# A hybrid recurrent, attention and Fourier stack on one core: scan normalisation by tokens, and dilated keys in sorted order

## The chip, the cores and the metric

The kernel runs on one core of a Trainium2 chip. The metric is the device time of the whole program in microseconds, from launch to the last store. TensorE multiplies matrices, VectorE, ScalarE and GpSimd do the rest, and SyncE queues transfers. The program is one long row of stages; each is a block of five instruction streams, one an engine, that wait for one another through semaphores. A stage starts on all engines when the one before has ended on all of them.

## The reference, cut to what matters

A first block on 2048 tokens of width 1024 (recurrent branch plus dilated attention), then a second block of two layers, on 2048 tokens and 256 context tokens. The change touches two computations.

The dilated attention has 8 heads of 64 channels and three patterns. Each works on every dilation-th token, in windows of 128 of those:

```python
DILATED_PATTERNS = ((128, 1), (512, 4), (2048, 16))
outs, lses = zip(*[dilated_attention(qh, kh, vh, w, d) for (w, d) in DILATED_PATTERNS])
wts = jax.nn.softmax(jnp.stack(lses, axis=0), axis=0)
att = jnp.einsum('pbhs,pbhsd->bhsd', wts, jnp.stack(outs, axis=0))
```

The scans of the second block (4 heads of 64 channels) end with a root-mean-square norm over each head's 64 channels, a gain, and a gate:

```python
def rms_norm_2(x, g):
    y = xf * lax.rsqrt(jnp.mean(xf * xf, axis=-1, keepdims=True) + EPS)
    return (y * g.astype(jnp.float32)).astype(x.dtype)
...
gain = hg_g.reshape(HG_HEADS, 1, HG_DV)
out_l = from_heads(rms_norm_2(o_lat, gain)).astype(q_l.dtype)
...
y = jnp.concatenate([y_conv, att_l * g_att, hg_l * g_hg, y_four], axis=-1) @ w_out
```

## The kernel before

Features lie on the 128 partitions, tokens along the free axis: `QT` and `KTt` (tiles `q_t` and `k_t` in the trace) are [128, 4, 2048], four pairs of heads, one head in each half of the partitions.

**stage_dilated** (lines 874 to 1127) works through `plan`, 96 units in a fixed order: 3 patterns x 16 query tiles of 128 x 2 groups of four heads. Units 0 to 31 are the pattern of dilation 1, 32 to 63 that of 4, 64 to 95 that of 16. A unit has `w` = 1 or 2 key blocks: two except for the first tile of each row of blocks, so 30, 24 and 0 units of the three patterns are 256 keys wide, the others 128. TensorE's order for unit u is written out: transpose the probabilities of u (`turn`, L1000), score matmuls of u + 2 (`scores`, L986), two matmuls of the second block's modulation (`modulate`, L1030), probabilities times values of u (`values`, L1017). In `scores` the queries are the stationary operand and the keys the moving one; both are read with the dilation as the step. VectorE masks and takes minima (L1058), copies transposed probabilities (L1068), adds modulation rows (L1078) and copies results out of PSUM (L1089) and, in every second unit, the statistics (L1088). ScalarE takes exponentials (L1111) and copies the other half of the transposes (L1121). GpSimd has no work. SyncE loads values (L935) and modulation weights (L942), stores result rows (L964) and modulation rows (L948), and brings back the recurrent branch's result into `yaT` (tile `ya_t`, L970), needed in the next stage only.

**stage_hgrn_norm** (lines 1930 to 1983) runs once in each layer, after the two scans. It cuts the output `oT` of [128, 2, tokens] into units of 512 tokens (`CH`): ten in layer 0, two of which have 256 tokens, and eight in layer 1. Per unit: ScalarE squares (L1949), TensorE multiplies by `headmean` (a 128x128 matrix of two 64x64 blocks of 1/64), which gives each channel its head's mean (L1964), ScalarE takes the root (L1956), VectorE the reciprocal (L1971) and the product with output and gain (L1973), GpSimd the product with the gate (L1981). Squares, roots and the PSUM tiles have two buffers each. The next stage begins with the projection of L2054.

## Time and profile before

| | us |
|---|---|
| three timed runs: median (lowest, highest) | 5314.19 (5302.58, 5317.26) |
| the profiled execution, and its span | 5306.81, 5304.8 |
| TensorE busy, share of the span | 4750.0, 90% |
| VectorE, ScalarE, GpSimd busy | 2483.5, 1688.8, 1208.3 |
| dilated attention, from and to | 808, 1223 |
| norm of the scans, layer 0, from and to | 2108, 2149 |
| norm of the scans, layer 1, from and to | 4031, 4068 |

The trace gives each instruction's start, duration and engine; an fp32 matmul shows as two weight loads (PEld) and two matmuls (PE). Ends of matmuls are modelled, so the pace of a row of them is read from one group's start to the next group's start, which is exact, and not from their durations, which overlap. A busy share says little by itself; what ends an engine's wait says more. The granted clock is TensorE's, as a share of 2.4 GHz: 1.00 is that level and 0.50 the lower one of 1.2 GHz.

### The profile page before, as it was taken

How to read it: one execution, taken by the hardware profiler on the slowest of the kernel's cores; microseconds unless marked ns; L12 is line 12 of the kernel's file. 1: busy time of each engine (PE TensorE's matmuls, PEld its weight loads, DVE VectorE, ACT ScalarE, POOL GpSimd, SP SyncE). 2: the span in 40 equal slices, each digit the busy share in tenths (PEclk: the TensorE clock that was granted, in tenths of full speed). 3: DMA queues.
4: the chain of work that ended last, by engine and by line, in shares of the span. 5: the costliest groups of instructions: out<-in, count | busy, mean ns of one | idle time of the engine just before them, and what ended most of it. 6: DMA issues, size and time to landing. Idle time of an engine off the chain costs nothing. (4 is left out here: it accounts for less than half of the span.)

```text
span 5304.8 us, 66741 instructions
## 1 busy us (share of the span) xinstructions
PE 4750.0 (90%) x26209; PEld 3269.9 (62%) x26209; DVE 2483.5 (47%) x4843; ACT 1688.8 (32%) x3122; POOL 1208.3 (23%) x1239
## 2 busy tenths in 40 slices
PE   6989998997969988899999898989896999988989
PEld 3447776775758655745554576876665644544767
DVE  3322345556643656635541264444566445501544
ACT  3332225553353111223441233242112234321431
POOL 1000020003410101418880001001122267830000
PEclk8989999998979999899999999999998999999999
DMA  5012104334420000100001202200000100002022
GB/s 190 8 56 72 40 1 158 133 104 162 149 99 17 1 9 1 57 17 11 11 9 38 72 16 92 88 28 17 9 1 31 36 9 13 7 25 86 16 72 95
DMA packets 149818, 272.41 MB, mean 51 GB/s; under 512 B 11645, under 2 KB 82693, under 8 KB 147845
## 3 DMA queue, kind: packets, MB, share of 16 engines
q1 hardware_dynamic: 145188, 257.67, 14.3%
q10 hardware_dynamic: 4320, 10.49, 0.5%
q8 instruction: 211, 3.46, 0.3%
q14 instruction: 99, 0.80, 0.1%
HBM read 198.92 MB, written 69.19 MB: 51 GB/s over the span
## 5 line engine op out<-in xcount | busy, mean ns | idle before, releaser
L1489 PE MATMUL ps_proj<-features_high,weights_high 128*128 128x512 f32 (+1 forms) x880 | 347.2, 394 | 60.6 <-DVE features_low L1552 31.2
L1489 PE MATMUL ps_proj<-features_high,weights_low 128*128 128x512 f32 (+1 forms) x880 | 341.1, 388 | 0.0
L1489 PE MATMUL ps_proj<-features_low,weights_high 128*128 128x512 f32 (+1 forms) x880 | 340.2, 387 | 0.0
L1703 PE MATMUL ps_s<-qf,kb 64*128 64x128 f32 x3264 | 235.7, 285 | 60.9 <-DVE scores_t L1873 55.5
L2436 ACT ACTIVATE weight_ring<-ps_st 128x1024 f32<-128x1024 f32 x193 | 197.9, 1025 | 249.1 <-PE ps_st L2323 243.2
L1703 PEld LDWEIGHTS ps_s<-qf,kb 64*128 64x128 f32 x3264 | 200.8, 188 | 112.6 <-issue 59.8
L1552 DVE TENSOR_TENSOR features_low<-h_t,features_high 128x1024 fp32r<-128x1024 f32 (+1 forms) x140 | 159.8, 1144 | 186.7 <-ACT features_high L1517 186.4
L2941 PE MATMUL ps_o<-w_out_high,y_high 128*128 128x512 f32 x544 | 217.4, 400 | 27.4 <-DVE y_low L2959 19.9
L1489 PEld LDWEIGHTS ps_proj<-features_high,weights_high 128*128 128x128 f32 x880 | 171.6, 195 | 110.0 <-DVE weights_low L1543 31.3
L2484 DVE TENSOR_REDUCE features_or_outputs<-ps_max 128x2 f32<-128x1024 f32 x128 | 156.7, 1224 | 166.0 <-PE ps_max L2293 166.0
L728 PE MATMUL ps_proj<-weights_high,features_high 128*128 128x512 f32 x512 | 207.0, 404 | 27.8 <-DVE features_low L823 27.8
L2466 POOL TENSOR_TENSOR features_or_outputs<-features_or_outputs,weight_ring 128x512 f32<-128x512 f32 x176 | 223.4, 1290 | 33.3 <-ACT weight_ring L2436 30.9
L2466 POOL TENSOR_TENSOR y_t<-y_t,weight_ring 128x512 f32<-128x512 f32 x176 | 223.3, 1290 | 33.3 <-ACT weight_ring L2436 30.9
L2484 DVE TENSOR_REDUCE y_t<-ps_max 128x2 f32<-128x1024 f32 x128 | 156.7, 1224 | 156.3 <-PE ps_max L2293 156.3
L1552 DVE TENSOR_TENSOR features_low<-features_or_outputs,features_high 128x1024 fp32r<-128x1024 f32 (+1 forms) x120 | 144.2, 1204 | 169.6 <-ACT features_high L1517 169.3
L1111 ACT ACTIVATE scores<-scores,row_stats 128x256 f32<-128x256 f32 (+1 forms) x384 | 172.4, 450 | 160.5 <-DVE row_stats L1058 160.5
L2941 PE MATMUL ps_o<-w_out_low,y_high 128*128 128x512 f32 x544 | 214.3, 394 | 0.0
L2941 PE MATMUL ps_o<-w_out_high,y_low 128*128 128x512 f32 x544 | 214.0, 393 | 0.0
L2318 PE MATMUL ps_st<-q_high,k_split 128*128 128x512 f32 x580 | 211.5, 446 | 0.0
L1873 DVE COPY_PREDICATED scores_t<-level_masks,ps_s 128x256 f32<-128x256 uint8 (+1 forms) x432 | 210.2, 560 | 0.0
L1517 ACT ACTIVATE features_high<-h_t 128x1024 fp32r<-128x1024 f32 (+1 forms) x140 | 136.1, 974 | 221.7 <-PE ps_proj L1489 190.7
L728 PE MATMUL ps_proj<-weights_high,features_low 128*128 128x512 f32 x512 | 204.8, 400 | 0.0
(428 smaller groups left out, 10542.7 us busy)
## 6 DMA issues: line engine op xcount, KB each, us to landing
weight_ring<-in_w_in_dram SPq DMA_DIRECT2D x40, 1024.0 KB, 5.6
weight_ring<-in_w_mod_dram SPq DMA_DIRECT2D x48, 512.0 KB, 4.1
t_rows<-t_rows SPq DMA_DIRECT2D x64, 256.0 KB, 2.3
x_res<-h_rows SPq DMA_DIRECT2D x32, 512.0 KB, 3.5
res<-result SPq DMA_DIRECT2D x48, 264.0 KB, 2.1
res_rows<-res SPq DMA_DIRECT2D x48, 264.0 KB, 3.8
h_t<-v_rows SPq DMA_DIRECT2D x3, 4096.0 KB, 13.9
q_rows<-q_rows SPq DMA_DIRECT2D x34, 256.0 KB, 2.6
```

Of the source, the lines that this page charges most:

```text
L728: mm = pe.matmul(out[:, :], f_[:, k, i * P:(i + 1) * P], w_[:, k0 + k, :], start=(k0 + k == 0 and n == 0), stop=(k0 + k == KT - 1 and n == 2))
L1111: act.activation(pr[:, u % 2, 2 * b + j, 0:w * P], sc[:, u % 2, 2 * b + j, 0:w * P], ACT.Exp, bias=stat[:, (u // 2) % 4, h:h + 1], scale=-1.0,
L1489: mm = pe.matmul(bank[:, 0:n], w_[:, k0 + k, i * P:(i + 1) * P], f_[:, k, 0:n], start=start, stop=stop)
L1517: act.activation(self.fh[:, s % NB, :, 0:n], self.hT[:, k0:k0 + KS, c0:c0 + n], ACT.Copy).then_inc(self.fhs.h, 1)
L1552: dve.tensor_tensor(self.fl[:, s % NB, :, 0:n], self.hT[:, k0:k0 + KS, c0:c0 + n], self.fh[:, s % NB, :, 0:n].bitcast(F32), ALU.subtract). ...
L1703: mm = pe.matmul(pS[pr][h][:, i * P:(i + 1) * P], kb[lo, s % 2, pr, i * P:(i + 1) * P], q, start=True, stop=True)
L1873: ins = dve.copy_predicated(dst, mask, src)
L2318: pe.matmul(sT[b][:, kv, :], KA[:, kv, ks], QA[g % 2][:, kv, :, :].rearrange("p i c -> p (i c)"), start=True, stop=False)
L2436: act.activation(pT[s % 3], sT[s % 2][:, :, :], ACT.Exp, scale=HD ** -0.5).then_inc(ex.h, 1)
L2466: pool.tensor_tensor(acc[g % 2][:, kv, :], before, pT[s % 3][:, kv, :], ALU.add).then_inc(pa.h, 1)
L2484: ins = dve.tensor_reduce(part[:, g % 2, t, c, :].rearrange("p (v i) -> p v i", v=2)[:, :, i], pM[:, :, 0:n], AXX, ALU.max)
L2941: mm = pe.matmul(ps[i % 2][half][:, :], y[:, i % 2, k, :], w[:, k, sl], start=(k == 0 and n == 0), stop=(k == KT - 1 and n == 2))
```

## The change

In **stage_dilated** GpSimd copies the keys into another order: for the pattern of dilation 4 from `KTt` into `yaT`, which is free at that time, with all tokens of one remainder next to one another; for dilation 16 from there back into `KTt`. `scores` reads a contiguous run of the sorted keys; the queries are read with a step, as before. TensorE waits for the first four copies ahead of unit 32 and for all eight ahead of unit 64. GpSimd waits with the second four for the last scores of dilation 1. The four loads into `yaT` move to units 69, 73, 77 and 81.

In **stage_hgrn_norm** the squares become the stationary operand and two columns of `headmean` the moving one, so that a matmul gives the means of 128 tokens, tokens on partitions, one column a head. All means of one channel pair (`pr`) go into one PSUM tile; one root and one reciprocal serve them all. ScalarE widens each value to 64 columns (`o_repeat`), and products with the identity put them back with channels on partitions. VectorE's multiply reads them from PSUM. The loops interleave the second pair's means with the first pair's spreading.

```diff
-                if u % 8 == 1 and 1 <= u // 8 <= CT:
-
-                    c = u // 8 - 1
+                c = u // 4 - NT - 1
+                if u % 4 == 1 and 0 <= c < CT:
+
+                    sp.wait_ge(kp.h, kp.at(8))
                     sp.dma_start(yaT[:, c, :], ya_d[:, c, :]).then_inc(yld.h, 16)
...
                 p, t, hh, (q0, dil), (k0, _), w, vt = plan[u]
+                if p >= 1 and u % (2 * NT) == 0:
+                    pe.wait_ge(kp.h, kp.at(4 * p))
+                k1 = (k0 % dil) * (S // dil) + k0 // dil
...
                                        QT[lo:lo + HD, pair, q0:q0 + dil * (P - 1) + 1:dil],
-                                       KTt[lo:lo + HD, pair, k0:k0 + dil * (w * P - 1) + 1:dil], start=True, stop=True)
+                                       KS[p][lo:lo + HD, pair, k1:k1 + w * P], start=True, stop=True)
...
+        @block.gpsimd
+        def _(pool):
+            for pr in range(4):
+                pool.tensor_copy(yaT[:, pr, :].rearrange("p (r i) -> p r i", r=4),
+                                 KTt[:, pr, :].rearrange("p (i r) -> p r i", r=4)).then_inc(kp.h, 1)
+
+            pool.wait_ge(smm.h, smm.at(2 * NT))
+            pool.wait_ge(kp.h, kp.at(4))
+            for pr in range(4):
+                pool.tensor_copy(KTt[:, pr, :].rearrange("p (a r i) -> p r a i", a=4, r=4),
+                                 yaT[:, pr, :].rearrange("p (r i a) -> p r a i", r=4, a=4)).then_inc(kp.h, 1)
...
 def stage_hgrn_norm(env, layer, oT, zT, chunks):
...
+        rr = env.sb(ctx, "o_rms", [P, 2, TN, 2])
+        re = env.sb(ctx, "o_repeat", [P, 2, CH // P, 2, HD])
+        pm = env.banks(ctx, "ps_mean", 2)
+        ps = env.banks(ctx, "ps_on", 4)
...
+        heads = env.headmean[:, 0:P:HD]
...
+            def root(pr):
+                act.wait_ge(mm_.h, mm_.at((pr + 1) * NC))
+                act.activation(rr[:, pr, :, :].rearrange("p t h -> p (t h)"), pm[pr][:, 0:2 * TN], ACT.Sqrt,
+                               bias=env.eps[:, :]).then_inc(rt.h, 1)
...
+            def repeat(u):
+                pr, (c0, n) = units[u]
+                m = n // P
+                act.wait_ge(rc.h, rc.at(pr + 1))
+                if u >= 2:
+                    act.wait_ge(bc.h, bc.at(u - 1))
+                act.activation(re[:, u % 2, 0:m, :, :].rearrange("p t h c -> p (t h) c"),
+                               rr[:, pr, c0 // P:c0 // P + m, :].rearrange("p t h -> p (t h)")[:, :, None].to_broadcast([P, 2 * m, HD]),
+                               ACT.Copy).then_inc(ex.h, 1)
+
+            for u in range(NC + 1):
+                square(u)
+            root(0)
+            for u in range(NC):
+                if NC + 1 + u < NU:
+                    square(NC + 1 + u)
+                repeat(u)
+            root(1)
+            for u in range(NC, NU):
+                repeat(u)
...
+            def means(u):
+                pr, (c0, n) = units[u]
                 pe.wait_ge(sq.h, sq.at(u + 1))
+                for j in range(n // P):
+                    t = c0 // P + j
+                    mm = pe.matmul(pm[pr][:, 2 * t:2 * t + 2], o2[:, u % 2, j * P:(j + 1) * P], heads, start=True, stop=True)
+                mm.then_inc(mm_.h, 1)
+
+            def spread(u):
+                pr, (c0, n) = units[u]
+                pe.wait_ge(ex.h, ex.at(u + 1))
+                if u >= 4:
+                    pe.wait_ge(sd.h, sd.at(u - 3))
+                for j in range(n // P):
+                    mm = pe.matmul(ps[u % 4][:, j * P:(j + 1) * P],
+                                   re[:, u % 2, j, :, :].rearrange("p h c -> p (h c)"), env.ident[:, :],
+                                   start=True, stop=True)
+                mm.then_inc(bc.h, 1)
...
             for u, (pr, (c0, n)) in enumerate(units):
+                if u % NC == 0:
+                    dve.wait_ge(rt.h, rt.at(pr + 1))
+                    dve.reciprocal(rr[:, pr, :, :], rr[:, pr, :, :]).then_inc(rc.h, 1)
                 o = oT[:, pr, c0:c0 + n]
-                dve.wait_ge(rt.h, rt.at(u + 1))
-                dve.reciprocal(rr[:, u % 2, 0:n], rr[:, u % 2, 0:n]).then_inc(rc.h, 1)
-                dve.wait_ge(rc.h, rc.at(u + 1))
+                dve.wait_ge(bc.h, bc.at(u + 1))
                 dve.scalar_tensor_tensor(out=o, in0=o, scalar=gains[:, 2 * layer + pr:2 * layer + pr + 1],
-                                         in1=rr[:, u % 2, 0:n], op0=ALU.mult, op1=ALU.mult).then_inc(sd.h, 1)
+                                         in1=ps[u % 4][:, 0:n], op0=ALU.mult, op1=ALU.mult).then_inc(sd.h, 1)
```

TensorE in the norm stage of layer 0, before (`ps_on` is the PSUM tile of the means, `o_sq` the squares):

```order
4050 L1958 UNCONDITIONAL_BRANCH
4051 L1964 MATMUL ps_on_146<-o_sq,head_mean 128x512 x4
4052 L1964 MATMUL ps_on_146<-o_sq,head_mean 128x256
4053 L1964 MATMUL ps_on_146<-o_sq,head_mean 128x512 x4
4054 L1964 MATMUL ps_on_146<-o_sq,head_mean 128x256
```

TensorE at the same place, after:

```order
4051 L2008 MATMUL ps_mean_147<-head_mean,o_sq 128x2 x30
4052 L2017 MATMUL ps_on_148<-ident,o_repeat 128x128 x4
4053 L2008 MATMUL ps_mean_147<-head_mean,o_sq 128x2 x4
4054 L2017 MATMUL ps_on_148<-ident,o_repeat 128x128 x4
4055 L2008 MATMUL ps_mean_147<-head_mean,o_sq 128x2 x2
4056 L2017 MATMUL ps_on_148<-ident,o_repeat 128x128 x28
```

Ten matmuls become 36 two columns wide and 36 of 128 columns; 30 of the former stand ahead of the first spreading product.

VectorE in the same stage, before (the first of ten such pairs):

```order
2076 L1971 RECIPROCAL o_rms<-o_rms 128x512
2077 L1973 SCALAR_TENSOR_TENSOR features_or_outputs<-features_or_outputs,vcols,o_rms 128x512
2078 L1971 RECIPROCAL o_rms<-o_rms 128x512
2079 L1973 SCALAR_TENSOR_TENSOR features_or_outputs<-features_or_outputs,vcols,o_rms 128x512
2080 L1971 RECIPROCAL o_rms<-o_rms 128x512
```

VectorE there, after:

```order
2076 L2036 RECIPROCAL o_rms<-o_rms 128x36
2077 L2039 SCALAR_TENSOR_TENSOR features_or_outputs<-features_or_outputs,vcols,ps_on_148 128x512 x4
2078 L2039 SCALAR_TENSOR_TENSOR features_or_outputs<-features_or_outputs,vcols,ps_on_148 128x256
2079 L2036 RECIPROCAL o_rms<-o_rms 128x36
2080 L2039 SCALAR_TENSOR_TENSOR features_or_outputs<-features_or_outputs,vcols,ps_on_148 128x512 x4
2081 L2039 SCALAR_TENSOR_TENSOR features_or_outputs<-features_or_outputs,vcols,ps_on_148 128x256
```

Ten wide reciprocals become two of 36 columns; the multiplies stay, with another second operand.

SyncE's queue in the dilated attention, before, around the first load into `ya_t` (units 7 to 11):

```order
60 L942 DMA weight_ring<-in_w_mod_dram 128x4x256
61 L964 DMA res<-result 128x528
62 L970 DMA ya_t<-ya_rows 128x2048
63 L942 DMA weight_ring<-in_w_mod_dram 128x4x256
64 L948 DMA mod_rows<-mod_rows 1x256 x4
```

SyncE's queue after, around the same load, now among the units of dilation 16:

```order
136 L944 DMA weight_ring<-in_w_mod_dram 128x4x256
137 L966 DMA res<-result 128x528
138 L973 DMA ya_t<-ya_rows 128x2048
139 L944 DMA weight_ring<-in_w_mod_dram 128x4x256
140 L950 DMA mod_rows<-mod_rows 1x256 x4
```

The load has the same neighbours, about 75 places further down the queue.

## Rows read from the trace of the kernel before

**Rows 1.** The page's first part: busy time, share of the span, instructions.

```profile
PE 4750.0 (90%) x26209; PEld 3269.9 (62%) x26209; DVE 2483.5 (47%) x4843; ACT 1688.8 (32%) x3122; POOL 1208.3 (23%) x1239
```

**Rows 2.** Busy time by stretch: stretch, length, engines, granted clock, DMA share, GB/s.

```profile
808.00:961.00 153.00, 142.87 (x1118) 112.33 (x1118) 86.36 (x372) 86.72 (x297) 0.00 (x0) 0.94 0.48 164
961.00:1119.00 158.00, 158.00 (x1053) 116.00 (x1054) 84.83 (x368) 78.99 (x288) 0.00 (x0) 1.00 0.34 114
1119.00:1223.00 104.00, 104.00 (x779) 79.34 (x777) 65.85 (x362) 60.54 (x281) 0.00 (x0) 1.00 0.37 117
2108.00:2149.00 41.00, 13.66 (x20) 3.87 (x20) 36.50 (x20) 12.48 (x21) 11.58 (x10) 0.67 0.00 0
4031.00:4068.00 37.00, 11.59 (x16) 3.07 (x16) 32.21 (x16) 10.93 (x17) 10.11 (x8) 0.63 0.00 0
```

**Rows 3.** TensorE's timeline, dilation 1: start, length, operation, tiles, shapes, count.

```profile
884.92 1.14 PE L986 MATMUL ps_score<-k_t,q_t 64*128 64x256 f32 x8
885.99 0.65 PE L1030 MATMUL ps_pv<-weight_ring 128*64 128x256 f32 x4
```

**Rows 4.** The same, dilation 4.

```profile
1021.18 2.19 PE L986 MATMUL ps_score<-k_t,q_t 64*128 64x256 f32 x8
1023.31 0.65 PE L1030 MATMUL ps_pv<-weight_ring 128*64 128x256 f32 x4
```

**Rows 5.** The same, dilation 16.

```profile
1181.54 1.23 PE L986 MATMUL ps_score<-k_t,q_t 64*128 64x128 f32 x8
1182.70 0.65 PE L1030 MATMUL ps_pv<-weight_ring 128*64 128x256 f32 x4
```

**Rows 6.** Weight loads of the scores, dilation 1, then 4: ns minimum/median/maximum.

```profile
L986 PEld LDWEIGHTS ps_score<-k_t,q_t x240: 182/187/334, 808.5 to 943.4; 64*128 64x128 f32 x120
...
L986 PEld LDWEIGHTS ps_score<-k_t,q_t x200: 304/307/329, 960.9 to 1077.4; 64*128 64x128 f32 x100
```

**Rows 7.** TensorE's timeline in a scan: same shape, both operands contiguous.

```profile
2101.13 1.16 PE L1703 MATMUL ps_s<-qf,kb 64*128 64x128 f32 x16 [1.29 <-ACT scores_t L1787]
```

**Rows 8.** Groups of layer 0's norm stage: busy us, mean ns, idle before.

```profile
L1971 DVE RECIPROCAL o_rms<-o_rms 128x512 f32<-128x512 f32 x8 | 26.8, 3347 | 3.5 <-ACT o_rms L1956 3.5
...
L1981 POOL TENSOR_TENSOR features_or_outputs<-features_or_outputs 128x512 f32<-128x512 f32 x8 | 10.1, 1267 | 55.6 <-DVE features_or_outputs L1973 55.6
L1973 DVE SCALAR_TENSOR_TENSOR features_or_outputs<-features_or_outputs,vcols,o_rms 128x512 f32<-128x512 f32 x8 | 6.0, 752 | 0.3
```

**Rows 9.** Timeline at the ends of the norm stages, layer 0, then 1.

```profile
2108.11 1.15 ACT L1949 ACTIVATE o_sq<-features_or_outputs 128x512 f32<-128x512 f32 x2 [3.67 <-PEq L1635]
...
2109.27 1.28 ACT L1956 ACT_TABLE_LOAD   x1
...
2149.30 5.98 PE L2054 MATMUL ps_proj<-weight_ring,h_t 128*128 128x256 f32 x18 [13.37 <-PEq L1935]
...
4031.00 1.15 ACT L1949 ACTIVATE o_sq<-y_t 128x512 f32<-128x512 f32 x2 [5.82 <-PEq L1635]
...
4068.36 6.89 PE L2054 MATMUL ps_proj<-weight_ring,features_or_outputs 128*128 128x256 f32 x24 [14.46 <-PEq L1935]
```

**Rows 10.** GpSimd's groups: the only operation 2048 columns wide.

```profile
L603 POOL TENSOR_TENSOR gate_i<-gate_i,xa_conv 128x2048 f32<-128x2048 f32 x4 | 18.1, 4531 | 236.8 <-ACT gate_i L577 236.8
```

**Rows 11.** Busy time by stretch, columns as in rows 2.

```profile
808.00:830.00 22.00, 11.87 (x60) 8.25 (x61) 6.12 (x34) 7.66 (x29) 0.00 (x0) 0.61 0.99 352
2120.00:2130.00 10.00, 5.22 (x6) 1.50 (x6) 9.89 (x7) 3.12 (x7) 3.52 (x4) 0.50 0.00 0
2149.00:2160.00 11.00, 10.71 (x41) 9.20 (x42) 1.77 (x6) 4.90 (x4) 1.56 (x2) 0.82 0.51 149
```

**Rows 12.** TensorE's timeline: one moving column, then 128, full stationary tiles.

```profile
223.90 3.63 PE L528 MATMUL ps_ss<-ones,gate_r 128*128 128x1 f32 x32
...
2973.11 3.81 PE L2650 MATMUL ps_t<-dft_t,t_rows 128*128 128x128 f32 x32
```

**Rows 13.** VectorE's copy of the statistics: ns minimum/median/maximum.

```profile
L1088 DVE COPY result<-row_stats x48: 166/168/170, 832.5 to 1224.3; 128x16 f32<-128x16 f32 x48
```

More of the change, by code:

```diff
@@ L1966, in _ @@
+            for u in range(NC + 2):
+                means(u)
+            for u in range(NC):
+                if u + NC + 2 < NU:
+                    means(u + NC + 2)
+                spread(u)
+            for u in range(NC, NU):
+                spread(u)
         @block.vector
```

38 lines of the change are left out of this document (14 added, 24 removed).

## Prediction

> **What bounds the kernel now.** I read the page's first part, then the busy time of each engine in the stretches that the change touches, then TensorE's timeline inside them. TensorE is busy 90% of the span [rows 1], so a saving counts in full only where TensorE never waits, or where another engine holds everybody up. The two edits lie in one place of each kind.
>
> The dilated attention runs from 808 to 1223 us. After an opening that waits for loads, TensorE is busy for every microsecond of it: 158 of 158 us in the second pattern (dilation 4), 104 of 104 in the third (dilation 16) [rows 2]. VectorE and ScalarE are busy for about half. So each microsecond taken from TensorE's stream there comes off the end, until another engine is the later one.
>
> The two norm stages of the scans (2108 to 2149 and 4031 to 4068 us) are the reverse: VectorE is busy 36.5 of 41 and 32.2 of 37 us, TensorE a third of it, much of that at the lower clock [rows 2]. The groups show why: a reciprocal of 128x512 takes 3.35 us, the multiply behind it 0.75 [rows 8]. Nothing of the next stage starts before the stage ends, so its whole length is on the path: from the first square at 2108.11 to the next projection at 2149.30, and from 4031.00 to 4068.36 [rows 9], 41.2 and 37.4 us.
>
> **Sorted keys, TensorE.** One unit is four score matmuls, eight instructions on the timeline. With contiguous keys 256 wide they take 885.99 - 884.92 = 1.07 us [rows 3]. With keys four apart, the same work takes 1023.31 - 1021.18 = 2.13 us [rows 4]. With keys 16 apart and 128 wide it is 1182.70 - 1181.54 = 1.16 us [rows 5]. Two operands are strided there: the keys (moving) and the queries (stationary). The change sorts only the keys. Which one sets the pace? The stationary side is 128 columns in [rows 4] and in [rows 5] alike, and its load takes 307 ns at the median against 187 without a stride [rows 6]; if it set the pace, both would take the same. They differ by 0.97 us, so the keys set it in [rows 4], and the strided query loads need at most 1.16 us a unit. So a 256-wide unit of pattern two falls from 2.13 to between 1.07 and 1.16: 0.97 to 1.06 us. There are 24 (12 tiles with two key blocks, two head groups): 23.3 to 25.5 us; I take 25.
>
> The other 8 units of pattern two and all 32 of pattern three are 128 wide. The best case is a row of another stage with the same shape and nothing strided: 16 instructions in 1.16 us, 0.58 for eight [rows 7], a saving of 0.58 a unit, 23 us in 40 units. The worst is that the strided query load already takes the 1.16: nothing. The load gets 120 ns longer by the stride [rows 6] at 128 columns, as many as the keys have in these units, so I expect the load to be about as late as the keys were, and take 0.05 a unit, 2 us. Sum for the stage: 27 us, with ends 23 and 48.
>
> The trace shows a doubled time for a stride of four floats and about the same per column for sixteen. The Trainium skill, SBUF — State Buffer, box on cachelines under "Door 1", says that reads are full speed only when consecutive accesses stay in a 16-byte line, and that four fp32 is the limit. The trace agrees that stride 4 is already past it; the page says nothing of which operand is the later one, and it does not change the sum.
>
> **Sorted keys, what is added.** GpSimd makes eight copies of 128x2048, on an engine that is idle for the whole stage [rows 2]. The nearest row, a 128x2048 multiply of two inputs, takes 4.53 us [rows 10]; one input could halve it, a stride could double it: 2.3 to 9 us, taken as 4.5. Four run at the stage's start, with 150 us until TensorE first waits for them (ahead of unit 32). Four wait for the last scores of pattern one and have some 130 us before unit 64. TensorE's two waits cost nothing unless a copy takes over 30 us. The four loads of the recurrent branch's result, 1 MB each, move on SyncE's queue from units 9 to 33 to units 69 to 81. Queued behind their new wait are the modulation weight loads and the result stores; the wait is long satisfied at unit 69. The third pattern's DMA share is 0.37 at 117 GB/s [rows 2]; 4 MB in 16 units of 3.2 us add 80 GB/s, and 352 GB/s at 0.99 were reached in the opening [rows 11]. Nothing, then; without that cover, a late weight load would cost a microsecond or two.
>
> **Norm stage, step by step.** Removed: ten (layer 1: eight) wide reciprocals and as many wide roots. Added, per 128x512 unit: four mean matmuls with the squares stationary and two columns moving, a widening copy on ScalarE, four 128x128 identity products. Each fp32 matmul is two instructions. Eight with a single moving column go at 3.63/32 = 0.113 us each, so 0.9 us a unit; eight of 128 columns at 3.81/32 = 0.119, so 0.95 [rows 12]; both twice that at half the clock. The squares take 0.58 us each [rows 9]. I walk layer 0 at the higher clock:
> - Squares and means of the first pair, 4.5 units: 0.6 + 4.5 x 0.9 = 4.6 us.
> - One more square 0.6, table load 1.28 [rows 9], root of 36 columns 0.25 and their reciprocal 0.3 (36 x 6.5 ns, scaled from the 3.35 us row [rows 8]): 6.9. A square and a widening copy: 8.1. TensorE has one more mean unit ahead of the first spread, so the spread runs 9.3 to 10.5, with its latency.
> - Then TensorE sets the pace: mean plus spread, 1.85 us a unit. Multiply of the fifth unit done at 16.0.
> - Second reciprocal 0.3, copy 0.6, spread 1.2, multiply 0.75, handovers: the gating multiply of GpSimd starts at 19.0 and sets the pace from there at 1.27 a unit [rows 8]: 4.5 units, 5.8. End at 24.9, and 0.3 for the change of stage.
>
> Before, from start to the next projection, it was 41.2 us: 16.0 saved. Layer 1 with eight equal units comes out at 22.3 + 0.3 against 37.4: 14.8. Together 31. If TensorE stays at the higher clock, the next stage also begins there: it now begins at the lower level (0.82 granted over its first 11 us [rows 11]), worth about 1.5 us in each layer. Norm stages: 34 us.
>
> **Sum.** 27 + 34 = 61 us. The profiled execution took 5306.8 us (span 5304.8); the three timed runs lie at 5302.6, 5314.2 and 5317.3, and the four average 5310. 5310 - 61 = 5249.
>
> **Rivals.**
> - *Queries not the later operand.* The stationary load is hidden and the 40 narrow units reach the contiguous rate: 20 us more, 5229. For: loads overlap matmuls everywhere. Against: unstrided, a load of 187 ns goes with a pace of 0.073 us an instruction [rows 6, 7]; one of 307 would have to keep that pace. Chance 0.15.
> - *Slow norm stages.* Either TensorE falls to the lower clock from the eleventh microsecond (about 31 and 27 us for the stages), or VectorE's and GpSimd's multiplies, which now run side by side, exclude each other (2.0 us a unit: 33 and 29). Either leaves 15 to 20 of 34 us: about 5265. For: today the clock falls to 0.50 in this stage [rows 11]. Against: it fell after 9 us of a TensorE that was a third busy; it would now be busy nine tenths of that time. Chance 0.2.
> - *GpSimd's copies hold VectorE, slower than before.* Every second unit VectorE copies statistics from SBUF to SBUF (0.17 us [rows 13]); if that waits out a GpSimd copy of length c, VectorE loses up to c. It has (153 - 86.4)/32, two microseconds a unit, of slack, some 4 a pair of units. Eight copies then cost 8 x (c - 4): nothing at 4.5 us, and the 61 us are gone from c = 11.6 on. At c = 13: 72 us, 5321. No row of this kernel has GpSimd that slow (2.5 times [rows 10]). Chance 0.03.
> - *One half does nothing.* Something not in the trace, such as a handover in the norm stage dearer than I think, leaves under 16 us: 5300. The step from [rows 3] to [rows 4] makes it unlikely. Chance 0.04.
>
> The third rival rests on a rule as well. The Trainium skill, SBUF — State Buffer, "Who interferes with whom", says that VectorE and GpSimd share a port pair, taken for a whole instruction by a VectorE copy in a two-port mode or one with two SBUF inputs. No row of this trace shows either being held. By that rule the multiply of the norm stage, which now reads one input from PSUM, is free of it.
>
> **How the numbers follow.** The forecast has 0.58. Its own spread is some 10 us each way: 23 to 28 in the dilated stage, 27 to 37 in the norms, and the runs' own. The range from 5226 to 5272 takes in the first two rivals and leaves about 0.15 outside. A comparison here tells about 0.3%, 16 us, from no change. Faster by more: 0.93; within: 0.04; slower: 0.03.
>
> **What would show it.** Right: the 256-wide scores of pattern two at 1.07 to 1.16 us for eight, the pattern in 132 us and not 158; narrow scores still near 1.1; norm stages of about 25 and 22.5 us, a GpSimd tail at 1.27 us a unit. Wrong: narrow scores near 0.6 (first rival); clock 0.50 in the norm stage or multiplies over 1 us there (second); TensorE idle in patterns one or two beside GpSimd copies over 9 us (third). If the wide scores stay at 2.13, the reading of which operand is late has failed.

## The result, and the profile after

| | before | changed |
|---|---|---|
| median of 11 runs each, us | 5309.49 | 5277.99 |
| lowest, highest | 5302.42, 5317.26 | 5267.05, 5298.84 |
| profiled execution, span | 5306.81, 5304.8 | 5298.84, 5296.8 |
| ratio, 95% interval | | 0.9937 (0.9926 to 0.9948) |

The changed kernel is 31.5 us faster; 61 were forecast, and 5278 lies above the range (5226 to 5272). Its profiled execution is the slowest of its eleven. One execution of e13 (further down) took 7436.8 us at a mean granted clock of 0.598, and its row leaves it out as a disturbed one. A step below is the time from the first score matmul of one unit of the dilated attention to that of the next; the table shows where the profiled spans differ, each stage taken from its first matmul to that of the next stage.

| stage | before | changed | forecast |
|---|---|---|---|
| dilated attention: the next stage's first matmul comes earlier by | | 17.6 | 27 |
| norm, layer 0, from the first square | 41.2 | 31.1 | 25.2 |
| norm, layer 1, from the first square | 37.4 | 28.8 | 22.6 |
| attention, layer 0 (code unchanged) | 507.1 | 520.3 | |
| attention, layer 1 (code unchanged) | 494.6 | 502.7 | |

The page of the changed kernel (busy us, share, instructions), for [rows 1]:

```profile
PE 4780.5 (90%) x26445; PEld 3322.8 (63%) x26445; DVE 2433.6 (46%) x4829; ACT 1688.6 (32%) x3126; POOL 1237.7 (23%) x1247
```

TensorE is busy for longer than before, though its stream got cheaper. The stretches of the three patterns and of the two norm stages show one place of this (length, then busy us and count of each engine, granted clock, DMA share, GB/s); they answer to [rows 2]:

```profile
812.00:961.00 149.00, 143.00 (x1118) 111.98 (x1116) 88.08 (x362) 83.44 (x287) 18.68 (x6) 0.94 0.40 136
961.00:1104.00 143.00, 139.64 (x1056) 114.77 (x1056) 85.28 (x378) 81.05 (x297) 7.71 (x3) 0.98 0.37 123
1104.00:1202.00 98.00, 98.00 (x754) 77.13 (x753) 62.62 (x356) 59.46 (x278) 0.00 (x0) 1.00 0.51 164
2090.00:2121.00 31.00, 24.87 (x144) 24.33 (x144) 7.46 (x13) 12.75 (x23) 11.24 (x10) 0.71 0.00 1
4025.00:4054.00 29.00, 23.01 (x128) 22.44 (x128) 6.67 (x11) 11.27 (x19) 10.02 (x8) 0.71 0.00 1
```

The middle pattern took 143 us and not 132: TensorE idles in it now, and the clock falls once. At the stage's start something else is new. VectorE's first copy, 0.43 us in the kernel before, takes 4.07 beside GpSimd's first copy of keys, and the first scores wait for it (before, then changed):

```profile
808.04 0.43 DVE L1091 COPY weight_ring<-c_silu 128x512 f32<-128x512 f32 x1 [4.31 <-PEq L668]
...
807.54 4.07 DVE L1109 COPY weight_ring<-c_silu 128x512 f32<-128x512 f32 x1 [3.69 <-PEq L668]
811.66 2.08 PE L992 MATMUL ps_score<-k_t,q_t 64*128 64x128 f32 x16 [5.06 <-DVE weight_ring L1109]
```

This costs nothing. Soon after, TensorE waits 4.8 us for modulation weights, where it waited 8.4 before, and unit 33 starts at 961.0 us in both kernels (960.86, 960.98). From first matmul to first matmul the stage is 20.8 us shorter (439.9, 419.2), but 3.1 of that is the later start; 17.6 came off its end. The scores themselves, on TensorE's timeline (start, length, line, tiles, count), for [rows 4, 5]:

```profile
1016.35 1.31 PE L992 MATMUL ps_score<-ya_t,q_t 64*128 64x256 f32 x8
1017.60 0.65 PE L1036 MATMUL ps_pv<-weight_ring 128*64 128x256 f32 x4
...
1180.30 1.14 PE L992 MATMUL ps_score<-k_t,q_t 64*128 64x128 f32 x8
1181.37 0.65 PE L1036 MATMUL ps_pv<-weight_ring 128*64 128x256 f32 x4
```

Wide scores go in 1.25 us (2.13 before), narrow ones in 1.07 (1.16). Steps are 4.63 us for 5.51 and 3.13 for 3.22; the contiguous ones of the first pattern are 4.46. Two steps behind unit 33 are worse than before. The first is from unit 33 to 34, 5.25 us for 4.19. GpSimd's and VectorE's rows there:

```profile
953.21 15.51 POOL L1060 COPY k_t<-ya_t 128x2048 f32<-128x2048 f32 x4 [130.32 <-PE ps_score L992]
957.50 3.54 DVE L1106 COPY result<-row_stats 128x16 f32<-128x16 f32 x1
960.96 0.41 DVE L1107 COPY result<-ps_pv 128x256 f32<-128x256 f32 x1
```

The copy of the statistics, 0.17 us in [rows 13], takes 3.54 while GpSimd copies keys at 3.9 us each. The second is from unit 42 to 43, 8.88 us for 5.51 before. TensorE at that place, first in the kernel before, where it does not wait, then changed:

```profile
993.62 2.19 PE L986 MATMUL ps_score<-k_t,q_t 64*128 64x256 f32 x8
995.74 0.65 PE L1030 MATMUL ps_pv<-weight_ring 128*64 128x256 f32 x4
...
992.64 1.31 PE L992 MATMUL ps_score<-ya_t,q_t 64*128 64x256 f32 x8
996.02 0.65 PE L1036 MATMUL ps_pv<-weight_ring 128*64 128x256 f32 x4 [2.07 <-DMA weight_ring<-in_w_mod_dram]
996.60 3.28 PE L1023 MATMUL ps_pv<-h_t,cos 128*128 128x64 f32 x16
999.67 1.92 PE L1006 MATMUL ps_pt<-ident,scores 128*128 128x128 f32 x8
```

TensorE waits 2.07 us for modulation weights, and what follows runs at about half the rate (the eight transposes of a unit in 1.85 us for 0.97), with the granted clock at 0.50 for 6.8 us.

In the norm stage of layer 0, in pieces of 5 us (columns as above), for [rows 11]:

```profile
2095.00:2100.00 5.00, 4.75 (x23) 4.66 (x23) 0.38 (x1) 3.68 (x7) 0.00 (x0) 0.50 0.00 0
2100.00:2105.00 5.00, 5.00 (x25) 5.00 (x25) 0.19 (x1) 1.58 (x4) 0.00 (x0) 0.50 0.00 0
2105.00:2110.00 5.00, 5.00 (x25) 5.00 (x26) 1.30 (x2) 1.43 (x3) 2.21 (x2) 0.52 0.00 0
2110.00:2115.00 5.00, 3.27 (x30) 3.08 (x29) 2.55 (x5) 2.06 (x5) 3.48 (x4) 1.00 0.01 2
```

TensorE is busy with one gap of 0.25 us, and at the lower level of 1.2 GHz: the clock fell 1.7 us after the first mean and came back 17.1 us later. It had been low already at the end of the scan, from 8.5 to 1.7 us ahead of the first mean (in layer 1 from 11.6 to 1.4), and back at 1.00 in between. Its timeline and GpSimd's, for [rows 9]:

```profile
2102.72 2.06 PE L2017 MATMUL ps_on<-ident,o_repeat 128*128 128x128 f32 x8
2104.56 1.71 PE L2008 MATMUL ps_mean<-head_mean,o_sq 128*128 128x2 f32 x8
2106.13 2.05 PE L2017 MATMUL ps_on<-ident,o_repeat 128*128 128x128 f32 x8
...
2115.45 5.62 POOL L2047 TENSOR_TENSOR features_or_outputs<-features_or_outputs 128x512 f32<-128x512 f32 x5 [1.06 <-DVE features_or_outputs L2039]
```

A spread and a mean unit take 2106.13 - 2102.72 = 3.41 us where 1.85 were forecast. GpSimd's last five units begin 25.1 us after the first square (19.0 forecast) and take 5.6 us (5.8 forecast).

### The profile page after: what moved, and what is told of

Read it like the earlier page. It is cut to its first block and busy times, and to the rows that moved or that the text cites. A ratio compares the mean times of both kernels' runs of the same rounds, so it can differ in the third digit from the quotient of the medians.

```text
span 5296.8 us, 67210 instructions
## 1 busy us (share of the span) xinstructions
PE 4780.5 (90%) x26445; PEld 3322.8 (63%) x26445; DVE 2433.6 (46%) x4829; ACT 1688.6 (32%) x3126; POOL 1237.7 (23%) x1247
```

## Experiments

All runs, each kernel beside the kernel before on the same chip. "Gain at 0.953" is the difference of two straight lines of time against the mean granted clock of a run, one through the runs of each kernel, read at 0.953. The clock is recorded to 0.001, and runs lie 1 to 4 us off their line, so with four to eight runs this gain is good to some microseconds only.

| run | median (runs) | kernel before | ratio, 95% | mean clock | gain at 0.953 |
|---|---|---|---|---|---|
| e1_keys_only | 5298.7 (12) | 5306.4 | 0.9982 (0.9971-0.9993) | 0.9504 | 22.6 |
| e2_norm_only | 5300.2 (11) | 5306.4 | 0.9988 (0.9978-0.9998) | 0.9531 | 9.0 |
| e3_norm_filled | 5301.1 (12) | 5306.4 | 0.9992 (0.9979-1.0004) | 0.9543 | 3.4 |
| e5_after_again | 5275.4 (7) | 5309.0 | 0.9934 (0.9918-0.9949) | 0.9527 | 31.0 |
| e6_v_in_quarters | 5283.1 (5) | 5309.0 | 0.9947 (0.9928-0.9966) | 0.9516 | 31.6 |
| e7_stats_by_scalar | 5283.6 (4) | 5309.0 | 0.9940 (0.9918-0.9961) | 0.9527 | 31.7 |
| e8_wide_means | 5284.5 (6) | 5309.0 | 0.9950 (0.9935-0.9966) | 0.9517 | 29.7 |
| e9_both_repairs | 5269.1 (6) | 5309.4 | 0.9922 (0.9907-0.9938) | 0.9545 | 35.2 |
| e10_pause_before_attend | 5277.8 (6) | 5309.4 | 0.9940 (0.9922-0.9957) | 0.9533 | 31.1 |
| e13_both_repairs_again | 5268.8 (5) | 5306.4 | 0.9929 (0.9915-0.9942) | 0.9538 | 37.1 |
| e14_after_third_time | 5282.3 (6) | 5306.4 | 0.9956 (0.9941-0.9970) | 0.9522 | 29.1 |
| e15_keys_unstrided_unsorted | 5288.6 (8) | 5306.4 | 0.9974 (0.9961-0.9988) | 0.9516 | 21.8 |

Three kernels had one run only: e4_queries_unstrided 5280.9, e11_fill_512 5289.2, e12_fill_256 5294.7. A single run says little here; they are read by their profiles.

**Each half alone: e1, e2.** The changed kernel with the norm stage of before, and the kernel before with the new norm stage.

> Only the sorted keys; the norm stages are those of before. Theory (the two halves add, and what the changed kernel's runs spread over comes from the norm stages or from chance): the dilated stage gains what it gained in the changed kernel, 17 to 18 us, so the median is 5292 (5288 to 5297) against 5309, and the runs spread as little as those of before (15 us). Rival (the sorted keys shift something that makes the later attention stages lose clock): attention stages that run slower than before by 5 us or more in each layer, a spread over 25 us, a median near 5300.

> Only the norm stages by tokens; the dilated stage is that of before. Theory: the norm stages take 31 and 29 us in place of 41 and 37, with the granted clock at 0.50 for most of them, a gain of 18 to 19 us; where the later attention stages keep their clock the time is 5288 to 5292, and the runs spread by 30 us because some of them do not. Rival (clock losses have nothing to do with this half): spread 15 us, median 5290.

The stages did what they do in the changed kernel (norm of e2: 30.2 and 28.0 us between first matmuls, 30.4 and 28.1 in the changed kernel). The medians gave 8 and 6 us, in sum 14 and not 31. In each kernel the time goes with the run's mean clock, 3.3 to 5 us for each 0.001, and at equal clock the halves give 22.6 + 9.0 = 31.6. The runs of e1 had the lowest mean clock of the table, 0.9504. So a saving on TensorE's stream can reach the median or go along with a lower clock. That the sum comes out at equal clock does not make each half right, because the mean clock is itself a result of the edit. In the profile of e2 the norm stages are 10.3 and 8.7 us shorter, 19 in all, for a gain of 9.0 at equal clock; in that of e1 the dilated stage ends 11.3 us earlier, for 22.6. What each half is worth by itself in the median stays open. e1 also showed the hold by GpSimd at its worst. VectorE and GpSimd:

```profile
957.51 11.50 POOL L1060 COPY k_t<-ya_t 128x2048 f32<-128x2048 f32 x3
957.89 7.31 DVE L1106 COPY result<-row_stats 128x16 f32<-128x16 f32 x1
```

VectorE's copy waited through two of GpSimd's, the step from unit 33 to 34 took 11.10 us, and the clock was at 0.50 for the next 13.7.

**The changed kernel again: e5, e14.** The same program, to see whether the first result or the sum of the halves was the accident.

> The changed kernel itself, once more, beside the kernel before and beside the next three. In the runs of the two halves (keys only 5298.7, norm only 5300.2, before 5306.4) the time goes with the mean granted clock of the run: a straight line through each kernel's runs gives, at the clock 0.953, 5309.6 for the kernel before, 5287.0 for the keys alone and 5300.6 for the norm alone, and for the changed kernel's first eleven runs 5276.8. Theory: the halves are worth 22.6 and 9.0, they add up, and the keys' half showed only 8 of it because its runs had a lower mean clock (0.950 against 0.954). Then this kernel is 30 to 34 us below the kernel before at the clock 0.953 and its median stays near 5278 (5270 to 5288). Rival: the halves' medians are what they are worth (8 and 6), and the first result came from other conditions: the median is then about 5292, 14 below the kernel before, and at the clock 0.953 it is less than 20 below.

> The changed kernel a third time, for the comparison with the run before this one. Its two medians so far are 5278.0 and 5275.4, 31.5 and 33.6 below the kernel before. Both theories expect 5274 to 5280, and in the profile steps of 6.5 us or more from unit 42 to 43 and of 5.2 us or more from unit 33 to 34.

The medians are 5275.4 and 5282.3, 33.6 and 24.1 below the kernel before beside them; the first was 5278.0. At equal clock the gains are 31.0 and 29.1, and the halves' sum of 31.6 agrees with them: the first result was no accident. The steps were 5.93 and 6.75 us in e5, 5.91 and 6.69 in e14. There TensorE's wait for the weights came without a fall of the clock, so 2.1 us of the 8.88 were the wait and another 2.1 the clock. At the step from unit 33 to 34 it is the other way round: there the clock fell for 3.4 us in e5 and in e14, and not in the first profile.

**Which stride costs what: e4, e15.** e4 is the changed kernel with the queries, too, read from contiguous columns; e15 is the kernel before with contiguous keys and no copies. Neither picks the columns that the attention needs, so their results are others; only the price of the stride is read from them.

```diff
-QT[lo:lo + HD, pair, q0:q0 + dil * (P - 1) + 1:dil],
+QT[lo:lo + HD, pair, t * P:(t + 1) * P],
```

> The changed kernel with the queries of the two dilated patterns also read without a step (128 neighbouring columns: another set of queries, so the attention result is another one). Nothing else changes. Theory (the strided query load sets the pace that is left): a 256-wide unit of dilation 4 falls from 4.63 to the 4.46 us of dilation 1, and a 128-wide unit of dilation 16 from 3.13 to about 2.65, since eight narrow score instructions then go at 0.58 us. Rival (something else, such as the order of the weight loads, sets it): both stay within 0.05 us.

> The kernel before, with the keys read from contiguous columns (wrong ones, so the output of the dilated attention is another), the queries with their stride, no copies by GpSimd and no moved load of ya. This is the price of the keys' stride by itself. Theory: a wide unit goes from 5.51 to 4.63 us and a narrow one from 3.22 to 3.13, as with the copies, every one of the 24 and 40 of them, and neither the step at unit 34 (4.1) nor that at unit 43 has a hole from GpSimd; the hole at unit 43 comes from the load of V meeting earlier units, so it stays: 6.5 to 9 us there. The stage ends 20 to 24 us earlier than in the kernel before. Rival: the hole at unit 43 was GpSimd's doing (the units came late to it by their delay at unit 34), and without the copies the step is 4.63.

TensorE in e4, a wide and a narrow unit:

```profile
1041.70 1.13 PE L992 MATMUL ps_score<-ya_t,q_t 64*128 64x256 f32 x8
1042.76 0.65 PE L1036 MATMUL ps_pv<-weight_ring 128*64 128x256 f32 x4
...
1174.93 0.72 PE L992 MATMUL ps_score<-k_t,q_t 64*128 64x128 f32 x8
1175.58 0.65 PE L1036 MATMUL ps_pv<-weight_ring 128*64 128x256 f32 x4
```

Wide steps 4.46 us, narrow 2.71. So the queries' stride still costs the changed kernel 0.17 us in a wide unit and 0.42 in a narrow one: with contiguous keys the strided query loads are the later side at either width. In e15 wide and narrow steps are 4.63 and 3.13, the same as with sorted keys, and the step from 33 to 34 is 4.09. The hole at unit 43, TensorE's wait for the weights, is there all the same:

```profile
992.79 1.31 PE L986 MATMUL ps_score<-k_t,q_t 64*128 64x256 f32 x8
996.18 0.65 PE L1030 MATMUL ps_pv<-weight_ring 128*64 128x256 f32 x4 [2.08 <-DMA weight_ring<-in_w_mod_dram]
996.77 2.00 PE L1017 MATMUL ps_pv<-h_t,cos 128*128 128x64 f32 x16
```

So that wait comes from units that arrive early at weights queued behind the 4 MB of the third V, not from GpSimd. In e4, whose units are the shortest, the same wait is 4.58 us and the step 12.08.

**The two holes (the hold at unit 33 and the wait at unit 43) mended: e6, e7, then both: e9, e13.** e6 issues that load as four pieces at units 35, 39, 43 and 47; e7 gives the copy of the statistics to ScalarE.

```diff
-                if u == 2 * NT + 3:
-                    load_v(2)
+                if u in (35, 39, 43, 47):
+                    x = (u - 35) // 4
...
+                    sp.dma_start(V[:, 0, 4 * x:4 * x + 4, :].rearrange("i r c -> i (r c)"), views[2][:, 2048 * x:2048 * (x + 1)])\
+                      .then_inc(vl[0].h, 16)
```

```diff
-                    dve.tensor_copy(res[:, (u // 2) % 2, H1 * HD:RW], stat[:, (u // 2) % 4, :])
...
+                        act.activation(res[:, i, H1 * HD:RW], stat[:, (v // 2) % 4, :], ACT.Copy).then_inc(sk.h, 1)
```

> The changed kernel with the third load of V (4 MB, one transfer) issued as four pieces of 1 MB, four units apart, from unit 35 on. Theory: at unit 42 TensorE waits 2.1 us for the modulation weights because that one transfer fills the DMA engines at 983 to 998 us of the span, and the granted clock then falls to 0.50 for 6.8 us. With the pieces apart the step from unit 42 to 43 is 4.6 to 5.6 us and not 8.9, the granted clock stays 1.00 from 990 to 1010, and the dilated stage takes 415 us and not 419. Rival: the same bytes are moved in the same stretch, a piece still stands ahead of the weights in the queue and the wait only changes its place: some step between units 35 and 50 is still longer than 7 us, and the stage takes 418 to 420.

> The changed kernel with the small copy of the row statistics (128x16, from SBUF to SBUF) issued by ScalarE and not by VectorE. Theory: it alone is held while GpSimd's copies of the keys run (3.5 us in the changed kernel, 7.3 us in the one with the keys alone, where the granted clock fell after it), and VectorE's other work there, which reads PSUM, is not. Then the step from unit 33 to 34 is 4.2 us as before the change and not 5.25 (11.10 with the keys alone), nothing of the small copies takes over 0.6 us, GpSimd's copies keep their 3.9 us, and the stage takes 418 us. Rival: whatever VectorE has queued beside GpSimd's copies is held, or ScalarE's copy is: the step stays at 5 us or more.

> The changed kernel with both repairs of the dilated stage: the third load of V in four pieces, and the row statistics copied by ScalarE. Theory: each took its own hole away when alone (the step from unit 42 to 43 came to 4.63 us from 8.88, the step from 33 to 34 to 4.08 from 5.25), so together the stage has both steps near 4.6 and 4.1, takes 413 to 414 us, and the units from 33 to 43 give a lead of 5.3 us over the changed kernel's profile. The whole at the clock 0.953 comes to about 5274 (5270 to 5278), against 5277 to 5279 for the changed kernel, which a median can hardly tell. Rival: the second unit that computes ahead of schedule only waits for the weights longer elsewhere, and the stage stays at 415 or more.

> The changed kernel with both repairs of the dilated stage, again, on one chip beside the changed kernel itself (the next run). Theory: the repairs are worth what the steps of the stage gave, 4.3 us at the step from unit 42 to 43 and 1.1 to 1.8 at the step from 33 to 34, 4 to 6 us in all, less where in other executions the weights arrive earlier. At the clock 0.953 this kernel is then 3 to 6 us below the changed kernel, and its ratio to the kernel before is near 0.992. Rival: only the profiled executions have these holes, and the two kernels lie within 2 us of each other.

In e6 the step from 42 to 43 is 4.63 us and TensorE waits for nothing from 990 to 1010. The step from 33 to 34 is still 5.78. In e7 the step from 33 to 34 is 4.08, and ScalarE's copy takes its normal time in the midst of GpSimd's:

```profile
954.63 15.59 POOL L1062 COPY k_t<-ya_t 128x2048 f32<-128x2048 f32 x4 [129.56 <-PE ps_score L994]
...
962.56 0.21 ACT L1145 ACTIVATE result<-row_stats 128x16 f32<-128x16 f32 x1
```

Each repair alone shows in its step and not in the median: 5283.1 and 5283.6, against 5275.4 for the changed kernel on the same chip, and 31.6 and 31.7 at equal clock against 31.0.

With both, in e9 (columns as above), TensorE is busy all through the second and third patterns, and at full clock:

```profile
958.00:1100.00 142.00, 142.00 (x1101) 117.25 (x1101) 83.76 (x363) 83.98 (x316) 13.54 (x4) 1.00 0.39 124
1100.00:1198.00 98.00, 98.00 (x754) 77.14 (x753) 62.63 (x341) 61.20 (x294) 0.00 (x0) 1.00 0.50 164
```

The stage takes 411.7 us (412.7 in e13) for 419.2. From unit 33 to 95 the kernel before needs 256.1 us, e9 231.6: 24.5 saved, all that the steps can give. On one chip, e13 stands at 5268.8 (5264.6 to 5276.3) and the changed kernel, e14, at 5282.3 (5277.8 to 5290.2): 13.5 us, 8 at equal clock. e9 had 5269.1. In these two profiles the dilated stage is 6.6 us shorter, 4.3 of it behind unit 33, where the repairs act, and the rest in the opening, which they leave alone. Most of what remains is attention in layer 1 (494.8 against 504.4 us), whose code is the same, see below. So 4.3 us of this are shown to be the repairs' own, in one pair of profiles. This is the fastest version here, 0.1 to 0.3% under the changed kernel's three medians.

**The norm's clock: e3, e8, e11, e12.** e3 adds two matmuls of the identity with 512 columns of squares to each chunk's means, e11 one to each of the first seven chunks (six in layer 1), e12 the same half as wide. e8 adds nothing, but gives each mean 28 moving columns.

```diff
+                    if j in (0, 2):
+                        pe.matmul(pf[:, 0:n], env.ident[:, :], o2[:, u % 2, 0:n], start=True, stop=True)
```

```diff
-        heads = env.headmean[:, 0:P:HD]
+        heads = env.headmean[:, HD - 14:HD + 14]
```

> The changed kernel with two more fp32 matmuls 512 columns wide in each full mean unit of the norm stages, into a PSUM bank that nobody reads: 0.9 us more TensorE work a unit at the higher clock. Theory (the clock falls because a stream of weight loads with two moving columns does not hold it, and that is what the norm stages lost): the granted clock stays at 1.00 through the mean phase, mean plus spread take 2.7 us a unit and not 3.4, the stages take 27 and 25 us and not 31 and 29, total 6 to 9 us less than the changed kernel in runs of like clock elsewhere. Rival (the clock falls anyway, for the gap around the root, or the pace is set by something else): the clock is still 0.50, the extra work costs its full time, the stages take 38 and 35 us.

> The changed kernel with means of 28 moving columns each (14 equal ones for each head) where it has 2; the root reads every fourteenth column, so no instruction is added. Theory: the granted clock falls to 0.50 in the norm stages because TensorE is busy with weight loads alone there, and it holds while columns move, as with the filling matmuls of the earlier run. Then the granted clock stays near 1.00 from 2090 to 2120, a mean takes 0.12 to 0.16 us and not 0.20, and the stages (first mean to next stage's first matmul) take 25 us (23 to 28) for 30.4 and 23 us (21 to 26) for 28.1. The whole gains 10 us at the same mean clock. Rival: 28 columns change nothing in what the clock does, it falls at the same place, and the stages stay within 1 us of 30.4 and 28.1.

> The changed kernel with one filling matmul of 128x512 (not two) beside the means of each of the first 7 chunks in the norm stages, and none beside spreads. Theory: the granted clock holds at 1.00 while the filling runs. The filling costs 0.94 us a chunk and a chunk of means at full clock 0.48, 1.4 us in all for 0.8 now, 4 us more over 7 chunks, and what it can win is the spreads' pace of 3.4 us, at three chunks, 1.5 us each, if the clock stays up through them: the first layer's stage takes 29 to 31 us for 30.4. Rival: the clock falls anyway as soon as the filling ends or during it, and the stage takes 33 to 35.

> The same with the filling half as wide (128x256, 0.47 us at full clock). Here the filling with the means is 0.95 us a chunk at full clock, nearly covered by ScalarE's square of 0.72. Theory: if it holds the clock, the first layer's stage takes 26 to 28 us for 30.4, the best of the fillings. Rival: it is too little, the clock falls at the same place as without it, and then the filling costs 0.94 us a chunk, and the stage takes 34 to 36 us.

Stretches of the norm stages, layer 0 and layer 1 (columns as above): e3, then e11, e12 (layer 0 only) and e8.

```profile
2092.00:2129.00 37.00, 31.36 (x180) 23.15 (x180) 7.43 (x12) 12.86 (x23) 11.17 (x10) 1.00 0.00 1
4012.00:4050.00 38.00, 33.34 (x160) 23.13 (x160) 6.60 (x10) 10.70 (x19) 9.74 (x8) 0.88 0.00 1
```

```profile
2096.00:2124.00 28.00, 22.50 (x158) 19.04 (x158) 7.42 (x12) 12.74 (x23) 11.00 (x10) 1.00 0.00 1
4019.00:4057.00 38.00, 33.08 (x140) 27.01 (x140) 6.59 (x10) 11.07 (x19) 9.71 (x8) 0.64 0.00 1
```

```profile
2096.00:2130.00 34.00, 29.38 (x158) 28.23 (x158) 7.42 (x12) 12.19 (x22) 11.00 (x10) 0.70 0.00 1
```

```profile
2093.00:2124.00 31.00, 24.94 (x144) 24.36 (x144) 7.43 (x12) 12.69 (x23) 11.34 (x10) 0.70 0.00 1
```

With fillings of 512 columns the clock held in layer 0, and e11's stage took 28.0 us for 30.4, though TensorE did more. In e3 a filling cost 0.94 us a matmul, as two instructions, twice what I had put, and the stage took 36.7. In layer 1 the same fillings did not keep it up: in e11 it fell 2.1 us into the stage and stayed for 27.3 (38.2 us). In e3 it was low from 11.3 us ahead of that stage to 9.2 us into it, and then stayed at 1.00 to its end (38.4 us). Half the filling (e12: 34.7 and 32.5) and wider means (e8: 30.5 and 28.1) did not stop the fall. So that the low clock is what lengthens the stage is shown; that it falls for lack of moving columns is not.

One difference between the two layers is on record. In layer 1 the scan ended with a low stretch in every profile. In layer 0 it did so in nine of the seventeen, and in none of the two where the filling held. Of the new norm stages, those with such a stretch ahead that ended 1.2 to 2.6 us before them fell again 0.8 to 2.2 us after the first mean. Those in layer 0 without one fell after 3.2 to 3.4 us, or, with the 512-column fillings, not until TensorE's work there was done. In two layer-1 stages (e3, e13) the low stretch ran on into the stage. So what TensorE did ahead of the stage is a rival to what it does in it, and no run separates the two. What decides the fall stays open, and no version here makes both stages faster. The changed kernel's own stage in layer 0 took 30.4 us in two profiles and 31.8 in the third, where the low stretch lasted 20.5 us and not 17.1.

**Attention, code unchanged: e10.** In the profile of the changed kernel the clock falls in both attention stages, each time behind TensorE's 1.5 us wait for VectorE's maxima:

```profile
4386.42 0.75 PE L2359 MATMUL ps_max<-k_split,q_high 64*128 64x512 f32 x2 [1.48 <-DVE y_t L2550]
4387.11 1.11 PE L2346 MATMUL ps_mix<-ident,q_rows 128*128 128x128 f32 x4
4387.87 1.20 PE L2384 MATMUL ps_st<-q_high,k_split 128*128 128x512 f32 x2
```

The four matmuls of L2346 behind the wait take 0.76 us; behind the same wait in the kernel before they take 0.41, and nothing falls there. A low stretch also begins just ahead of each attention stage, in TensorE's 6.4 us wait for q_rows. How far ahead differs. In layer 1 it began 5.6 to 5.9 us before the first matmul in eight profiles, and all eight had falls in the stage (497 to 504 us); it began 6.7 to 7.4 before in seven, which had none (494.6 to 494.9). e15, where that stretch lasted 13.7 us for 10.2, had one fall (499.2). Layer 0: 5.7 to 6.2 with falls in five and without in one, 6.4 to 7.2 without in ten and with one in one. e10 adds one matmul behind that wait, in layer 1.

```diff
+                if g == 0 and t == 0 and not with_ctx:
+                    pe.matmul(px[:, 0:2 * P], env.ident[:, :], qd[:, 0:2 * P], start=True, stop=True)
```

> The changed kernel with one more matmul of 128x256 (its result is written over) ahead of the first one of the second layer's attention stage, right behind TensorE's wait for q_rows. In the profiles so far this stage took 502.7 to 503.0 us, with the granted clock falling three or more times in it, wherever the low stretch ahead of it began 5.6 to 5.9 us before its first matmul (5 kernels with both halves of the change), and 494.6 to 494.8 where it began 7.1 to 7.4 us before it (the kernel before, the keys alone, the norm filled). Theory: the falls behind the 1.49 us waits for the maxima hang on how the waits lie in time against what went before, and not on the work of the stage. The added matmul moves the stage by about 0.95 us, its low stretch then begins 6.8 us before it, no clock falls in the stage, and it takes 496 us with the added matmul in it; the whole is 6 us faster at the end. Rival: the falls come from something else that the change altered, and the stage takes 503.6 us (502.7 and the added matmul).

```profile
4171.66 1.19 PE L2346 MATMUL ps_mix<-q_rows,ident 128*128 128x256 f32 x2 [6.26 <-DMA q_rows<-q_rows]
4172.65 1.06 PE L2348 MATMUL ps_mix<-ident,q_rows 128*128 128x128 f32 x4
```

The stage took 496.0 us, with the added matmul in it and no fall, for 502.7: more work, and 6.7 us faster. The low stretch began 5.7 us before the added matmul and 6.7 before the first one of the old order. The edit moved the stage's later waits by a microsecond, but it also gave TensorE a microsecond of work where it had none, and it is one profile. That the falls hang on when the waits come fits it and the seventeen profiles, and is not shown by itself. The whole did not get clearly faster in the median: 5277.8, between the 5275.4 and 5282.3 of the changed kernel's repeats. What the falls are worth in other executions isn't settled.

## Why the prediction was wrong, by its steps

- **Wide scores.** The keys were the later side, as read from [rows 4, 5]: e15 alone gives the 0.88. The bound was wrong: "the strided query loads need at most 1.16 us a unit" came from narrow units of stride 16. The eight narrow units of stride 4 take 1.23 us in the kernel before, 1.13 in the changed one, and with stride 4 beside 256 columns the eight instructions take 1.25. The saving is 0.88 in each of 24 units, 21 us for the 25 taken.
- **Narrow units.** 0.09 to 0.10 in 40 units, 4 us for 2. That strided loads are about as late as the keys was right; e4 prices them, 0.42 a narrow unit. The first rival is out.
- **Sum of the stage.** 21 + 4 = 25 was there to have (24.5 in e9), for 27. The changed kernel got 17.6.
- **"TensorE's two waits cost nothing", and what lies behind them.** They did cost nothing. What I did not follow was the rest of the queues once TensorE runs ahead: the kernel before needed the modulation weights of this unit at 995.7 us, and they had come at 995.2, half a microsecond earlier; the changed one is ready for them at 993.9, and they come at 996.0, behind the 4 MB of V, a load that the change does not touch. From their place in the queue to their arrival they take the same in both (14.8 and 14.6 us); it is TensorE that needs them after 12.5 us and no longer after 15.3. That is 2.1 us, and 4.2 where the clock falls too.
- **GpSimd's copies hold VectorE.** The mechanism of the third rival is real, at 3.84 to 3.94 us a copy (4.5 taken). Its price, c - 4, was taken from the mean slack of the first pattern; by that formula eight copies of 4.5 us cost 4 us, and the text put nothing. The second four copies run into the change from wide to narrow units, where a 3.54 us hold already costs 1.2 us, and one of 7.31 us, through two copies, 7. The first four hold VectorE too, for 4.07 us at the stage's start, which a wait for weights covers. The Trainium skill, SBUF — State Buffer, "Who interferes with whom", has the lock on the pair of ports that these two engines share, taken for a whole instruction, and says that ScalarE never waits for it. The trace agrees on both engines (VectorE's copy 3.54 us, ScalarE's 0.21 us in e7). In e1 the engine that was held waited out two of the other's instructions in a row (7.31 us).
- **Norm stage.** This is the larger failure. The pieces were right at full clock: root 0.29 and reciprocal 0.38 (0.25 and 0.3 taken), product 0.75, GpSimd's tail 5.6 us. The step that failed is "if TensorE stays at the higher clock": 34 us were forecast and 10.1 + 8.6 = 18.7 came. The second rival had the mechanism and nearly the sizes, 31 and 27 us for 31.1 and 28.8 measured; it was held down to 0.2 because TensorE would be busy nine tenths of the time. It was, and the clock fell all the same. That the sizes met is partly luck: the rival had the clock low from the eleventh microsecond on, and it was low from the third to the twentieth. The walk also had the order of the stream wrong. It put one mean unit of the second pair ahead of the first spread and one beside each later one; the kernel puts 60 of the 72 mean instructions ahead, so its 1.85 us a unit can hold for one and a half units only. And its 16.0 does not follow from that pace: 10.5 and three and a half units are 17.0 before the multiply. Each is a slip of a microsecond or so, and neither explains the 6 us by which each stage is late. Nor did the next stage's 3 us come (140.4 to 141.4, 133.2 to 133.5).
- **Place by place** the forecast had 27 + 34 = 61 and got 17.6 + 10.1 + 8.6 = 36.3. The median gained 31.5. In the profiled execution the two attention stages gave back 21 us of it and one output stage 5.5 (231.1 to 236.6); in the median it is some 5, the difference of 36.3 and 31.5. That unchanged stages could give anything back was in none of the rivals, and why they do stays open.

## What to carry to other kernels

A stretch that makes TensorE the bound by removing waits still has to be priced at both clock levels, and a full TensorE is no assurance of the higher one. When a stage gets faster, walk every queue again with the new times, the transfers that the edit does not touch too: e6 got 2.1 to 4.2 us of a step back by cutting up a load of the kernel before. Put small SBUF copies on ScalarE while GpSimd copies, as e7 did. And compare versions a few tenths of a per cent apart by several profiles, stage by stage, beside the medians. A comparison at equal mean clock helps, but it hides what the edit itself does to the clock.

## What the hardware showed that was not expected

- A strided stationary operand held the pace back at either width, and less beside a wider moving one: 0.19 us at 256 columns and 0.48 at 128. With contiguous keys eight score instructions take 1.25 us at 256 wide with queries 4 apart and 1.06 with contiguous ones; at 128 wide they take 1.13 with queries 4 apart, 1.07 with queries 16 apart and 0.65 with contiguous ones.
- VectorE's copy of 128x16 from SBUF to SBUF took 0.17 us, 3.54 beside GpSimd's copies and 7.31 in e1; its copies out of PSUM beside them kept 0.41.
- The granted clock fell to 0.50 1.7 us after a row of weight loads and two-column matmuls began, and stayed there with TensorE busy 4.75 to 5.00 of each 5 us. In e11, extra matmuls of 512 columns went with 1.00 in one stage and not in its twin, where a low stretch had ended 1.3 us ahead.
- A wait of 2.1 us for weights was followed by 6.8 us at the lower clock in one execution of the changed kernel and by none in two others.
